# Layer A of a fused network kernel: group 0 in order of time, two key chunks, shares joined later

## The reference, cut to what matters

```python
DILATED_PAIRS = ((128, 1), (512, 4), (2048, 16))    # (window, dilation); reach = window // 2 // dilation = 64
...
    out = einsum(exp(logits - mx), v) / denom
    return out, mx + log(denom)
...
alpha = softmax(stack(lses), axis=0)                # over the three groups
y = sum(alpha[..., None] * stack(outs), axis=0)
return (y * silu(gate)) @ w_out
```

## Time and profile before

| | |
|---|---|
| three runs | 1673.16, 1675.14, 1675.73 us (median 1675.14) |
| profiled execution | 1674.71 us |
| its span | 1672.9 us |
| mean granted TensorE clock | 0.978 of full speed |
| PE busy | 1568.7 us, 94% of the span |
| DVE, ACT, POOL busy | 755.5, 775.8, 788.4 us |
| bytes moved | 135.44 MB, mean 81 GB/s |

### The profile page before, as it was taken

One profiled execution on the slowest core, in us unless ns is written; L12 is line 12 of the kernel. 1 busy time (PEld: TensorE's weight loads), 2 busy tenths in 40 slices (PEclk: granted clock), 3 DMA queues, 4 the chain that ended last, 5 costly groups with the idle time before them and its releaser, 6 DMA issues. The chain is left out here.

```text
span 1672.9 us, 29914 instructions
## 1 busy us (share of the span) xinstructions
PE 1568.7 (94%) x11850; PEld 1271.6 (76%) x11850; DVE 755.5 (45%) x1630; ACT 775.8 (46%) x1436; POOL 788.4 (47%) x475
## 2 busy tenths in 40 slices
PE   6899999999999998989999998998968999899997
PEld 4788888888888886767777776676757887678876
DVE  4224342434434345334454334189436764265535
ACT  4534536363635444346656643245764343352222
POOL 4734425261624342456555543325647652375551
PEclk9999999999999999989999998999988999999999
DMA  7423232232323230254554213432000001333331
GB/s 180 120 59 94 71 96 80 76 101 67 101 70 104 74 90 1 63 149 139 143 154 134 76 51 88 115 70 63 26 28 3 4 3 28 88 89 101 90 92 57
DMA packets 247185, 135.44 MB, mean 81 GB/s; under 512 B 24390, under 2 KB 241518, under 8 KB 246999
## 3 DMA queue, kind: packets, MB, share of 16 engines
q1 hardware_dynamic: 220824, 109.12, 23.5%
q10 hardware_dynamic: 26224, 24.42, 5.2%
HBM read 131.00 MB, written 2.52 MB: 80 GB/s over the span
## 5 line engine op out<-in xcount | busy, mean ns | idle before, releaser
L919 POOL TENSOR_TENSOR a_sq_low<-a_sq,a_sq_high 128x512 fp32r<-128x512 f32 x48 | 62.1, 1293 | 278.4 <-ACT a_sq_high L766 278.4
L318 PE MATMUL a_proj<-h_low,w_high 128*128 128x512 f32 x472 | 190.0, 402 | 1.6 <-POOL h_low L938 0.8
L899 POOL TENSOR_TENSOR w_low<-a_w_raw,w_high 128x1024 fp32r<-128x1024 f32 x64 | 158.5, 2477 | 65.8 <-ACT w_high L733 65.8
L320 PE MATMUL a_proj<-h_high,w_high 128*128 128x512 f32 x472 | 185.7, 393 | 0.0
L319 PE MATMUL a_proj<-h_high,w_low 128*128 128x512 f32 x472 | 184.8, 392 | 0.0
L899 POOL TENSOR_TENSOR w_low<-b_w_raw,w_high 128x1024 fp32r<-128x1024 f32 x40 | 100.4, 2512 | 97.1 <-ACT w_high L733 97.1
L318 PE MATMUL b_proj<-h_low,w_high 128*128 128x512 f32 x288 | 116.5, 405 | 1.4 <-POOL h_low L938 0.8
L320 PE MATMUL b_proj<-h_high,w_high 128*128 128x512 f32 x288 | 113.5, 394 | 0.0
L319 PE MATMUL b_proj<-h_high,w_low 128*128 128x512 f32 x288 | 113.2, 393 | 0.0
L819 ACT ACTIVATE a_pt<-a_turned 128x512 f32<-128x512 f32 x64 | 37.8, 591 | 155.8 <-PE a_turned L612 155.8
L318 PEld LDWEIGHTS a_proj<-h_low,w_high 128*128 128x128 f32 x472 | 88.8, 188 | 23.4 <-DVE a_qk L969 3.2
(11 more groups left out here) (488 smaller groups left out, 4202.2 us busy)
## 6 DMA issues: line engine op xcount, KB each, us to landing
a_w_raw<-in_a_w_in_dram SPq DMA_DIRECT2D x78, 512.0 KB, 3.7
b_w_raw<-in_b_w_in_dram SPq DMA_DIRECT2D x30, 512.0 KB, 4.1
b_ada_w<-in_ada_w_dram ACTq DMA_DIRECT2D x24, 512.0 KB, 3.7
f_wt<-in_w_in_dram SPq DMA_DIRECT2D x19, 512.0 KB, 3.8
a_bias<-scr_a ACTq DMA_DIRECT2D x16, 576.0 KB, 4.7
sparse_w_raw<-in_w_in_dram SPq DMA_DIRECT2D x17, 512.0 KB, 3.8
a_w_raw<-in_a_w_out_dram SPq DMA_DIRECT2D x8, 512.0 KB, 3.6
b_w_raw<-in_b_w_out_dram SPq DMA_DIRECT2D x8, 512.0 KB, 3.6
```

The source lines that it names most:

```text
L318: nc.tensor.matmul(out, lh, rl, start=first, stop=False)
L320: return nc.tensor.matmul(out, lh, rh, start=False, stop=last)
L899: nc.gpsimd.tensor_tensor(low(slot_of(b)), raw[:, n % RAW, :, :], high(slot_of(b)), ALU.subtract).then_inc(s_wl, 1)
L919: nc.gpsimd.tensor_tensor(sql[:, :], sq[:, u % 2, :], sqh[:, :], ALU.subtract).then_inc(s_sql, 1)
```

## The change

`layer_a` and the general `attention_layer(nc, T, I, a)` are replaced by `layer_a_space` and an own function, `dilated_attention`. Layer B is still done by `attention_layer`.

- Group 0's q, k and V are kept in order of time. The keys are rolled by 16 within the time order so that a query tile of 128 tokens needs two key chunks, t and t+1. For this, `take` of the group 0 q is 4 DVE instructions, and that of k is 2 with a write stride of 4 elements.
- V of group 0 is now an eighth 512-token unit (V0), copied to `vfm`, and turned by four transposes in a thirteenth unit (VT). The four V units carry 256 columns, groups 1 and 2.
- A step has four chunks of 128 per head: 12 score instructions for t < 3 and 16 for t = 3, 8 transposes in one group, 16 instructions of the V product.
- Group 0 and groups 1 and 2 have different query orders, so each step has two softmax parts of 256 columns per head, each with its own peak and sum. `swap` carries peaks and sums over to the other order with 8 small DVE instructions per step, `shares` joins all of them once a pair (8 DVE and one ACT instruction), and `normal` scales by the share. All four steps' scores come first, then the shares, then transposes and V products.
- The gate's sigmoid is Exp, Ln, Exp on ACT; before it was Exp on ACT and add, reciprocal on DVE.
- The bias table is 896 instead of 2304 columns wide. Per head four DMAs (128, 32, 32 and 128 KB) are issued by SP, right behind the weight load that follows unit 5's.
- V weight blocks are split after units 4 and 5 instead of 1, 3 and 5.
- The output product's first three blocks (EARLY = 3) are worked on in the last pair. `Y` of a pair is written once.

```diff
+    V_AFTER = (4, 5)
+    HEAD_BANKS = [0, 1, 2, 3, 4, 5, 6, 0, 1, 2, 3, 1, 0]
+    PERIOD = [("S", 0), ("u", 0), ("S", 1), ("u", 1), ("S", 2), ("u", 2), ("S", 3), ("u", 3), ("C", 0), ("u", 4), ("u", 5),
+              ("T", 0), ("u", 6), ("A", 0), ("T", 1), ("u", 7), ("A", 1), ("T", 2), ("u", 8), ("u", 9), ("A", 2), ("T", 3),
+              ("u", 10), ("u", 11), ("A", 3), ("u", 12)]
+    LAST = [("S", 0), ("e", 0), ("S", 1), ("e", 1), ("S", 2), ("e", 2), ("S", 3), ("e", 3), ("C", 0), ("e", 4), ("e", 5), ("e", 6),
+            ("T", 0), ("f", 0), ("f", 1), ("A", 0), ("T", 1), ("f", 2), ("f", 3), ("A", 1), ("T", 2), ("f", 4), ("f", 5),
+            ("A", 2), ("T", 3), ("f", 6), ("A", 3), ("e", 7), ("f", 7)]
...
+            bias_after = {place["ring", NR * p + 5 + RING]: p for p in range(PAIRS)}
+            for n in range(RAW, len(order)):
+                sp.wait_ge(s_wl, n - RAW + 1)
+                load(n)
+                if n in bias_after:
...
+                    for h in range(2):
+                        load_bias(2 * bias_after[n] + h)
...
+            def scores(p, t):
...
+                near = [(0, t * P, WIN)] if t < 3 else [(0, t * P, P), (P, 0, P)]
+                for g, c0, k0, w in [(0, *n) for n in near] + [(1, WIN, t * P, P), (2, WIN + P, t * P, P)]:
+                    for h in range(2):
...
+            for p in range(PAIRS):
+                for kind, i in plan(p):
+                    if kind == "S":
+                        exps(p, i)
+                    elif kind == "C":
+                        weights(p)
+                    elif kind == "T":
+                        keep_pt(p, i)
+                    elif kind == "u":
+                        if 1 <= i <= NQK:
+                            inv_norm(p + 1, i - 1)
+                        after_projection(p + 1, i)
+                    elif kind == "e":
+                        y_high(i)
...
+            def swap(p, t):
+
+                dve.wait_ge(s_exp, 4 * (4 * p + t + 1))
+                for b in range(4):
```

More of the change, by code:

```diff
@@ L44 @@
 REL = 256
-A_ROWS = 9
-A_BIAS = A_ROWS * P
+A_NEAR = 3 * P
+A_TABLE = A_NEAR + 2 * REL
 GRID_ROWS, GRID_W = 8, 64
@@ L112, in buckets_c @@
         return np.where(dist < exact, dist, np.minimum(large, 31))
-    pick_a = np.zeros((33, A_ROWS, REL))
+    pick_a = np.zeros((33, A_TABLE))
+    for x in range(A_NEAR - 1):
+        rel = x - 191
+        pick_a[int(buckets_a(np.int32(rel))) if abs(rel) <= 64 else 32, x] = 1
     for x in range(REL - 1):
         d = x - 127
[L118 to L125, removed]
+        pick_a[int(buckets_a(np.int32(4 * d))) if abs(d) <= 64 else 32, A_NEAR + x] = 1
+        pick_a[int(buckets_a(np.int32(4 * d))) if d % 4 == 0 else 32, A_NEAR + REL + x] = 1
     pick_c = np.zeros((33, C_REL))
@@ L132, in shape_constants @@
     return {"k_consts": side(general), "k_rwkv": side(parts), "k_band": f(band),
-            "k_pick_a": f(pick_a.reshape(33, -1)), "k_pick_c": f(pick_c)}
+            "k_pick_a": f(pick_a), "k_pick_c": f(pick_c)}
 SHAPE_CONSTANTS = shape_constants()
@@ L180, in stage_in @@
         A, B, C, TREL = range(4)
-        pieces = [[(0, A, pick_a, 0, 0, 512), (1, A, pick_a, 512, 0, 512), (2, A, pick_a, 1024, 0, 512),
-                   (3, A, pick_a, 1536, 0, 256), (3, B, pick_a, 1792, 256, 256)],
-                  [(0, C, pick_a, 2048, 0, 256), (1, TREL, pick_c, 0, 0, 512), (2, TREL, pick_c, 512, 0, 128)]]
+        pieces = [[(0, A, pick_a, 0, 0, A_NEAR), (1, B, pick_a, A_NEAR, 0, REL), (2, C, pick_a, A_NEAR + REL, 0, REL),
+                   (3, TREL, pick_c, 0, 0, 512)],
+                  [(0, TREL, pick_c, 512, 0, C_REL - 512)]]
         PARTS = 4
@@ L199, in _ @@
                         sp.dma_start(T.norm_gain[:, n, :], src.rearrange("(k p) -> p k", p=P)).then_inc(s_ng, 16)
-                sp.wait_ge(s_rows, 4)
+                sp.wait_ge(s_rows, 5)
                 scr_a = I["scr_a"]
[L202 to L206, removed]
+                for g, c0, w in ((0, 0, A_NEAR), (1, A_NEAR, REL), (2, A_NEAR + REL, REL)):
+                    sp.dma_start(scr_a[:, c0:c0 + w], rows[32 * g:32 * g + HEADS, 0, 0:w]).then_inc(T.s_scr, 16)
+                sp.dma_start(I["scr_c"][:, 0:512], rows[96:104, 0, :]).then_inc(T.s_scr, 16)
+                sp.dma_start(I["scr_c"][:, 512:C_REL], rows[0:8, 1, 0:C_REL - 512]).then_inc(T.s_scr, 16)
                 sp.wait_ge(s_bq, 8)
@@ L281, in _ @@
                 act.wait_ge(s_rowmm, 1)
-                nc.scalar.activation(rows[:, 0, :], ps_rows[:, 0, :], ACT.Copy).then_inc(s_rows, 1)
+                for g, w in ((0, A_NEAR), (1, REL), (2, REL), (3, 512)):
+                    at = slice(32 * g, 32 * g + 32)
+                    nc.scalar.activation(rows[at, 0, 0:w], ps_rows[at, 0, 0:w], ACT.Copy).then_inc(s_rows, 1)
                 split_high(0)
                 act.wait_ge(s_rowmm, 2)
-                for g, w in ((0, 256), (1, 512), (2, C_REL - 512)):
-                    at = slice(32 * g, 32 * g + 32)
-                    nc.scalar.activation(rows[at, 1, 0:w], ps_rows[at, 1, 0:w], ACT.Copy).then_inc(s_rows, 1)
+                nc.scalar.activation(rows[0:32, 1, 0:C_REL - 512], ps_rows[0:32, 1, 0:C_REL - 512], ACT.Copy).then_inc(s_rows, 1)
                 split_high(1)
@@ L739, in _ @@
                 split_high(b)
-            act.wait_ge(T.s_scr, 128)
+            act.wait_ge(T.s_scr, 96)
             for head in range(L.bias_heads):
@@ L1122, in _, with layer_a_space @@
             add_square(nc, dve, T, sq, s_nsq, s_acc, KT - 1)
-def layer_a(T, I):
+def layer_a_space(T, I):
     L = Space()
[L1129 to L1133, removed]
+    L.w_in, L.x, L.index = "a_w_in", T.X0, 0
     width = HEADS * HD
@@ L1136, in layer_a @@
                              else ((i - 7) * 3 + 2) * width) + p * P
[L1137 to L1161, removed]
@@ L2809, in build @@
         T.causal = part("causal")
-        a, b = layer_a(T, I), layer_b(T, I)
+        a, b = layer_a_space(T, I), layer_b(T, I)
         w_in = I["w_in_2"][0].rearrange("(k p) n -> p k n", p=P)
@@ L2816, in build @@
         retire(nc, T)
-        attention_layer(nc, T, I, a)
+        dilated_attention(nc, T, I, a)
         retire(nc, T)
```

508 lines of the change are left out of this document (505 added, 3 removed).

## The result

The changed kernel takes 1723.62 us (median, 1722.79 to 1725.80) beside 1674.94 for the kernel before on the same chip: ratio 1.0294, 95% interval 1.0276 to 1.0312, slower. The prediction, 1672 with 1653 to 1689, was wrong, and the time lies outside its range. The profiled execution has a span of 1721.5, 48.6 more than before.

The account below looks back on a forecast made before the run. TensorE, busy 94% of the span, was taken as the bound. PE's work -29, new wait +14, head -6 and last pair +18 gave -3 us from 1674.71, so 1672 us; range 1653 to 1689.

Parts of the forecast that it names:

- PE's work per pair: Layer A's seven pairs: TensorE's work falls 4.5 us a pair, with 256-column matmuls at 0.120 us; -29 us in all.
- Rival C: TensorE's 256-column matmuls stay near 0.17 us, as stationary loads set a floor: +36 on the sum, 1705 us; chance 0.05.
- The new wait: Before A0, ACT waits for the second V block behind eight bias DMAs: 2.0 us a pair (0.6 to 4), +14.
- rival B: Second V block lands 21 us or more after u3, holding ACT between unit 5 and T0: 1688 us; chance 0.22.
- The clock behind the stall: Seven pairs: no slow clock counted behind the stall; half clock was taken only in the last pair, +7 us.
- DVE's slack: Seven pairs: DVE busy some 34 of 72 us, taking u3 0.5 us before PE wants u5; no stall counted.
- The head: Before the first pair: S0 comes at 90.3 instead of 96.66 us, -6.4, range -8 to -3.
- The last pair: Last pair: 8.4 us per step as each e waits on an uncovered chain, +11, half clock +7; total +18.

## Why the prediction was wrong, point by point

| term (us) | predicted | measured | from |
|---|---|---|---|
| PE's work, seven pairs | -29 | -28.6 | 506.86 busy undisturbed, 535.43 before |
| stall before A0, with its slow clock | +14 | +48.1 | 564.85 against 516.80 |
| other waits, 8.8 of it behind DVE | 0 | +9.9 | 516.80 against 506.86 |
| head | -6 | +2.3 | S0 at 98.97 against 96.66 |
| last pair | +18 | +15.0 | 63.74 against 48.8 |
| the rest of the span | 0 | +1.9 | 48.6 less the above |

- **PE's work per pair: right.** A run of 48 matmuls of 256 columns takes 5.64 or 5.83, 0.1175 to 0.1215 each (0.120 said), and the full cut of 28.6 us is there once nothing stands in its way. Rival C is out (by its own terms it stands at 1707, not 1705).
- **The new wait: the right place, a third of the size.** This is the step that failed, in the sentence "eight bias DMAs, at 0.37 each until 14.2". The load of u5's block was foretold 11.2 after u3's end and came at 11.4. The eight issues took 6.0 instead of 3.0, and the second V block reached ACT 5.4 after its issue at 17.8, not 4.8 after one at 14.2: 23.2 instead of 19. Undisturbed it goes out at 13.7, so my eight issues cost it 0.5, and the real ones 4.1. The row I used was that of a weight load. The trace before had nearer ones, which I did not look up: the issues of its own bias DMAs, on ACT's queue, reached 1.92 us (median 0.37), and one run of eight short fetches stood in SP's queue at

```profile
1046.71 5.13 SPq L1312 DMA_DIRECT2D sparse_table<-scr_c  x8
```

  which is 0.64 each on the mean (by single rows, the first took 1.74 and the other seven 0.43 to 0.46). None of these rows says how long a bias issue would take, but they would have given the constant an upper bound. At 0.64 the block lands 2.2 later and the stall is 4.2 a pair, rival B's case.
- **The clock behind the stall: left out.** I counted it in the last pair and not here. An idle stretch of 4.8 us cost 2.2 more a pair, 15.3 in all. In the run with half of the issues ahead, 2.9 us cost 1.4 more (516.71 busy against 506.86); the waits of 1.25 alone cost nothing (clock 1.00). So rival B's mechanism came true and its price, 1688, was also too low: it allowed 4 at one for one, and it was 6.9.
- **DVE's slack: too thin, and wrongly excluded.** I had u3's take 0.5 us early for u5 and counted no stall; it was 1.25 late. The hold of 2.1 by POOL's subtraction accounts for more than the difference of 1.75, and where it was taken away the wait before u5 went. No part of my queue arithmetic let two engines hold each other.
- **The head: -6 predicted, +2.3 measured.** The same eight issues again (6.6 us there), and the wait of 5.6 that follows. With them behind V, S0 comes at 90.07, and I had said 90.3.
- **The last pair: right.** Idle gaps of 5.0 to 5.1 before each of the first four e's name POOL's low part, steps are 9.0 to 9.9 (8.4 to 10.1 said), clock 0.79. But the terms as I wrote them add up to 8.2 a step, not 8.4, and T, A and f to 12.3, not 12.5. And not all bursts were slow: each e behind a gap ran at 0.50, while the scores took 1.15 and 1.19 for S0 and S1, then 1.79 and 2.08. How the 15.0 splits into chain and clock was not measured.

The range failed because the stall's upper bound, 4, was built from landing times while the issue time stood as a constant without bounds. The same constant was in two terms, so both missed in one direction.

## What to carry to other kernels

Price a DMA's issue on its queue by rows of the same kind of transfer, not by a weight load's, and bound it; then ask which load stands behind the group, and put the group behind the load that someone waits for. Where an in-order engine has a split that waits for a DMA ahead of a short copy that TensorE needs, a stall costs more than its own length once the clock falls behind it: here 4.8 us cost 2.2 more and 2.9 cost 1.4 more, while 1.25 cost nothing on top. In a stretch without cover, look for the one instruction that closes the loop between engines, and issue it earlier.

## What the runs showed of the hardware that I had not expected

- An issue of a bias DMA (32 or 128 KB) in the change kept SP for 0.5 to 0.8 us among the first four of a group of eight and for up to 1.8 among the later four; in the run with four on either side, the first two right behind the V block's load took 1.8 to 2.9 each. A load of 512 KB mostly took 0.37 or 0.47, but 1.74 in the head of the change, where it was the second one behind the eight. So the kind of transfer is not all of it, and what is still outstanding may be the rest; that was not tested.
- DVE operations of 0.15 to 0.34 us that work on SBUF alone (two tensor inputs, or the scaling of 256 columns) stand for 1.24 to 2.60 us when they meet a POOL subtraction, and end with it to within 0.15 us. Peaks that read PSUM keep their 0.42, and scalings of one column their 0.14. The mean over a group hides this; only single rows show it.
- It goes the other way too. In the staging, DVE had begun a row of eight subtractions at 32.52, until 37.4, and POOL's subtraction took 5.38 us instead of 2.4. The trace before has a row of 5.38 there as well, which could have led me to the rule:

```profile
34.30 5.38 POOL L1576 TENSOR_TENSOR w_low<-a_w_raw,w_high 128x1024 fp32r<-128x1024 f32 x1 [6.71 <-ACT w_high L1470]
```
